# Routing of a mixture of experts: router products on tiles as they arrive, first gather ahead of the branch, a weight ring of seven

## The reference

```python
def moe_swiglu(h, w_router, b_router, w_gate, w_up, w_down):
    logits = (h @ w_router).astype(F32) + b_router.astype(F32)
    top_logits, top_idx = lax.top_k(logits, TOP_K)          # TOP_K = 2
    top_w = jax.nn.softmax(top_logits, axis=-1)
    gates = jnp.sum(jax.nn.one_hot(top_idx, N_EXPERTS, dtype=F32) * top_w[..., None], axis=-2)
    out = jnp.zeros(h.shape, F32)
    for e in range(N_EXPERTS):                              # N_EXPERTS = 8
        y_e = swiglu(h, w_gate[e], w_up[e], w_down[e]).astype(F32)   # 1024 -> 3584 -> 1024
        out = out + gates[..., e:e + 1] * y_e
    return out.astype(h.dtype)
```

## Time and profile before

| | |
|---|---|
| time, median of 3 runs | 2658.06 us (2654.54 to 2659.94) |
| profiled execution, own time | 2662.36 us |
| its span, first to last instruction | 2660.5 us |
| TensorE busy | 2539.8 us, 95% |
| VectorE, ScalarE, GpSimd busy | 72%, 55%, 7% |
| granted TensorE clock, mean over the span | 0.972 |
| memory traffic | 567.60 MB, mean 213 GB/s |

### The profile page before, as it was taken

How to read it: one execution, slowest core, us unless ns; L and a number is a source line. 1 busy time by engine, 2 the same in 40 slices (tenths; PEclk the granted TensorE clock), 3 DMA queues, 4 the chain that set the end, 5 groups by cost and what they waited for, 6 DMA issues and landing times.

```text
span 2660.5 us, 39011 instructions
## 1 busy us (share of the span) xinstructions
PE 2539.8 (95%) x15929; PEld 2257.1 (85%) x15929; DVE 1921.7 (72%) x2436; ACT 1473.6 (55%) x1801; POOL 183.8 (7%) x201
## 2 busy tenths in 40 slices
PE   7998989999989899999999999999899999898998
PEld 6766989999879788888888888888798899887998
DVE  7885366544666588989898988988775775576773
ACT  2222355434465277777777777777635564435653
POOL 0000012212010100000000000000000121100120
PEclk9988999999999999999999999999999999999999
DMA  7221044554424299999999999999762455251551
GB/s 224 85 95 48 1 153 136 190 177 158 143 66 157 67 341 381 349 351 363 367 368 333 372 361 364 350 376 360 266 199 75 143 181 184 84 186 64 187 180 46
DMA packets 339048, 567.60 MB, mean 213 GB/s; under 512 B 17576, under 2 KB 184724, under 8 KB 338740
## 3 DMA queue, kind: packets, MB, share of 16 engines
q1 hardware_dynamic: 325942, 556.29, 59.7%
q10 hardware_dynamic: 12926, 8.77, 1.2%
HBM read 563.97 MB, written 2.24 MB: 213 GB/s over the span
## 4 chain that ended last, share of the span: by engine, by line
PE 86%; DVE 7%; ACT 4%; issue 2%; ACTq 0%; DMA 0%; POOL 0%; DVEq 0%; POOLq 0%
PE bank L206 23%; PE bank L208 22%; PE bank L207 22%; PE bank L2060 3%; DVE chunks_lo L326 2%; ACT chunks_hi L318 2%; PE bank L3217 1%; PE bank L1748 1%; PE bank L1731 1%; PE bank L645 1%; PE bank L2606 1%; PE bank L2593 1%; PE bank L2607 1%; PE bank L2112 1%; PE bank L2052 1%
## 5 line engine op out<-in xcount | busy, mean ns | idle before, releaser
L3345 DVE TENSOR_TENSOR weight_lo<-ring,weight_hi 128x2048 fp32r<-128x2048 f32 x336 | 766.8, 2290 | 112.1 <-ACT weight_hi L3280 110.2
L3280 ACT ACTIVATE weight_hi<-ring 128x2048 fp32r<-128x2048 f32 x336 | 643.5, 1918 | 208.1 <-PE bank L208 204.2
L326 DVE TENSOR_TENSOR chunks_lo<-ring,chunks_hi 128x2048 fp32r<-128x2048 f32 x175 | 403.2, 2304 | 300.6 <-ACT chunks_hi L318 300.4
L206 PE MATMUL bank<-x_parts,chunks_hi 128*128 128x256 f32 x1568 | 454.8, 290 | 21.9 <-DVE x_parts L409 13.7
L318 ACT ACTIVATE chunks_hi<-ring 128x2048 fp32r<-128x2048 f32 x175 | 333.8, 1908 | 229.9 <-PE bank L208 225.4
L207 PE MATMUL bank<-x_parts,chunks_hi 128*128 128x256 f32 x1568 | 447.6, 285 | 0.0
L208 PE MATMUL bank<-x_parts,chunks_lo 128*128 128x256 f32 x1568 | 447.3, 285 | 0.0
L206 PE MATMUL bank<-weight_hi,xg_parts 128*128 128x512 f32 x896 | 353.2, 394 | 1.0 <-DVE xg_parts L3351 1.0
L208 PE MATMUL bank<-weight_hi,xg_parts 128*128 128x512 f32 x896 | 349.3, 390 | 0.0
L207 PE MATMUL bank<-weight_lo,xg_parts 128*128 128x512 f32 x896 | 349.0, 390 | 0.0
L206 PEld LDWEIGHTS bank<-x_parts,chunks_hi 128*128 128x128 f32 x1568 | 304.3, 194 | 27.1 <-issue 17.1
(11 more groups left out here) (525 smaller groups left out, 4633.8 us busy)
## 6 DMA issues: line engine op xcount, KB each, us to landing
ring<-in_moe_w_gate SPq DMA_DIRECT2D x112, 1024.0 KB, 6.8
ring<-in_moe_w_up SPq DMA_DIRECT2D x112, 1024.0 KB, 6.8
ring<-in_moe_w_down SPq DMA_DIRECT2D x112, 1024.0 KB, 6.9
ring<-in_w_up SPq DMA_DIRECT2D x44, 1024.0 KB, 5.1
ring<-in_w_in SPq DMA_DIRECT2D x24, 1024.0 KB, 5.5
ring<-in_w_down SPq DMA_DIRECT2D x22, 1024.0 KB, 4.9
ring<-in_xa_w_kv SPq DMA_DIRECT2D x16, 1024.0 KB, 5.7
ring<-in_da_w_qkv SPq DMA_DIRECT2D x12, 1024.0 KB, 5.2
```

What stands on the lines that cost most here:

```text
L206: pe.matmul(dst, l[0], r[0], start=first, stop=False, skip_group_check=True)
L326: dve.tensor_tensor(self.lo[:, n % SPLITS], ring[:, c.slot], self.hi[:, n % SPLITS].bitcast(F32), ALU.subtract).then_inc(self.rest.sem, se ...
L3280: act.activation(weight_hi[:, slot(m, odd + next_)], ring[:, m % RING], ACT.Copy)\
L3345: dve.tensor_tensor(weight_lo[:, at_], ring[:, m % RING], weight_hi[:, at_].bitcast(F32), ALU.subtract)\
```

## The change

- The router products take each scaled tile as it is ready and stand ahead of the transposes; the row sums follow them. The scaling itself moves from VectorE to ScalarE, ahead of its square (`carry_hi`).
- The four tables are loaded by ScalarE's queue after its first square of the output product.
- `end_phase()` between the routing and the experts goes. VectorE's subtraction for `xt_lo` moves behind the slots and the crowd flag. TensorE gathers the first pair, upper parts, shares, lower parts, before it loads the flag and branches; ScalarE splits two chunks and copies the gathered tokens before it does; each waits for a semaphore `crowd_known` first.
- In every pair the share products stand behind the upper gather instead of ahead of it, with one more count.
- `RING` is 7 and `SCRATCH` 2048 columns shorter. The experts use six slots (`ROUND`); the seventh holds the lower parts of the gathered tokens. GpSimd's memsets of spare columns go.

```diff
-RING = 6
+RING = 7
-        SCRATCH = 35648
+        SCRATCH = 33600
...
         def carry_hi(act, n, gain, plain):
-            if not plain:
-                act.activation(x_parts[:, 0, n], h[:, n], ACT.Copy, scale=gain(n)).then_inc(x_hi.sem, x_hi.tick())
+            act.activation(x_plain[:, n] if plain else x_parts[:, 0, n], h[:, n], ACT.Copy, scale=gain(n))\
+               .then_inc(x_hi.sem, x_hi.tick())
...
                     carry_square(act, n)
+                    if n == 0 and early is not None:
+                        early(act)
...
             def _(pe):
-                pe.wait_ge(*ready(DT - 1))
+                pe.wait_ge(consts_in.sem, consts_in.total)
+                pe.matmul(bank[6][:, 0:E], ones[0:1, :], row_b[0:1, :], start=True, stop=True)
+                for k in range(DT):
+                    pe.wait_ge(x_hi.sem, arrived + k + 1)
+                    for t in range(TT):
+                        mm = pe.matmul(bank[4 + t][:, 0:E], x[:, k, t * P:(t + 1) * P], wr[:, k], start=k == 0,
+                                       stop=k == DT - 1)
+                mm.then_inc(routed.sem, routed.tick())
+                sum_x(pe, full=False, rows=True)
                 for n in range(4):
                     t, half = divmod(n, 2)
                     for m in range(4):
                         mm = pe.transpose(bank[n][:, m * P:(m + 1) * P], x[:, 4 * half + m, t * P:(t + 1) * P], ident[:])
                     mm.then_inc(turned.sem, turned.tick())
-                pe.wait_ge(consts_in.sem, consts_in.total)
-                pe.matmul(bank[6][:, 0:E], ones[0:1, :], row_b[0:1, :], start=True, stop=True)
-                for t in range(TT):
-                    for k in range(DT):
-                        mm = pe.matmul(bank[4 + t][:, 0:E], x[:, k, t * P:(t + 1) * P], wr[:, k], start=k == 0,
-                                       stop=k == DT - 1)
-                    mm.then_inc(routed.sem, routed.tick())
-                sum_x(pe, full=False, rows=True)
                 pe.wait_ge(chosen.sem, chosen.at(1))
-                pe.wait_ge(rested.sem, rested.at(4))
...
-            end_phase()
...
-            xg_parts = take_parts("xg_parts", 2, DT, T)
+            ROUND = RING - 1
+            xg_parts = [take_parts("xg_hi", DT, T),
+                        nc.alloc_sbuf_tensor_at("xg_lo", [P, DT, T], F32R, offset=ring_at + 4 * ROUND * CHUNK)]
...
             @block.tensor
             def _(pe):
+                pair_wait(pe, one_hot, 0, 1)
+                gather(pe, 0, FIRST_HI)
+                pair_wait(pe, fetched, 0, 1)
+                shares(pe, FIRST_HI[0])
+                pe.wait_ge(rested.sem, rested.at(4))
+                gather(pe, 1, FREE)
+                pe.wait_ge(crowd_known.sem, crowd_known.at(1))
                 many = crowded(pe)
...
             @block.scalar
             def _(act):
+                act.wait_ge(turned.sem, turned.at(4))
+                for m in range(2):
+                    upper(act, 0, m, 0)
+                tokens_in(act, 0, range(4), FIRST_HI, FIRST_HI[0])
+                act.wait_ge(crowd_known.sem, crowd_known.at(1))
                 many = crowded(act)
...
             @block.vector
             def _(dve):
+                dve.wait_ge(counted.sem, counted.at(3))
+                make_slots(dve, 0)
+                ordered(dve, dve_own, dve.tensor_reduce(crowd[:, 1:2], count, AX_X, ALU.max))
+                dve.tensor_copy(crowd[:, 0:1].bitcast(mybir.dt.int32), crowd[:, 1:2]).then_inc(crowd_known.sem, crowd_known.tick())
+                for n in range(4):
+                    t, half = divmod(n, 2)
+                    c_ = slice(half * 512, (half + 1) * 512)
+                    dve.wait_ge(copied.sem, copied.at(n + 1))
+                    dve.tensor_tensor(xt_parts[1][:, t, c_], bank[n][:, :], xt_parts[0][:, t, c_].bitcast(F32), ALU.subtract)\
+                       .then_inc(rested.sem, rested.tick())
+                dve.wait_ge(crowd_known.sem, crowd_known.at(1))
                 many = crowded(dve)
```

More of the change, by code:

```diff
@@ L402, in carry_lo @@
         def carry_lo(dve, n, gain, plain):
[L404 to L407, removed]
+            if not plain:
                 dve.wait_ge(x_hi.sem, x_hi.at(n + 1))
@@ L2853, in moe @@
             eq, one, two, two_l = (take(TT, E) for _ in range(4))
-            pick_, gates_, place_ = take(TT, E + 1), take(TT, E + 1), take(TT, E + 1)
-            pick, gates, place = (v_[:, :, 0:E] for v_ in (pick_, gates_, place_))
-            scaled_gates = take(TT, E + 1)
+            pick, gates, place, scaled_gates = (take(TT, E) for _ in range(4))
             choice, share = take(TT, 2, 2), take(2, 2)
@@ L2906, in _ @@
             def _(act):
-                act.wait_ge(consts_in.sem, consts_in.total)
+                root_x(act, full=False, rows=True)
                 for n in range(4):
@@ L2932, in _ @@
                 dve.tensor_scalar(minus[:], ident[:], -1.0, None, ALU.mult)
[L2933 to L2939, removed]
+                dve.wait_ge(routed.sem, routed.at(1))
                 o(dve.tensor_copy(row_l, bank[6][:, 0:E]))
@@ L3013, in moe @@
             UP = 4 * NB
-            assert NC % RING == 0
-            per_slot = NC // RING
-            views = [ring[:, m % RING, :].rearrange("p (a b) -> p a b", a=4 if m < UP else 2) for m in range(NC)]
+            assert NC % ROUND == 0
+            per_slot = NC // ROUND
+            views = [ring[:, m % ROUND, :].rearrange("p (a b) -> p a b", a=4 if m < UP else 2) for m in range(NC)]
             one_hot, weights_hi, weights_lo, y_left, y_rest = (
@@ L3186, in gather, with shares, tokens_in, upper @@
                     mm.then_inc(gathered.sem, 1)
-            FREE, FIRST_LO = (0, 1, 2, 3), (4, 5, 6, 0)
+            def shares(pe, b):
+                for q in range(2):
+                    for t in range(TT):
+                        mm = pe.matmul(bank[b][:, 2 * q:2 * q + 2], to_slot[:, t, q * P:(q + 1) * P].bitcast(F32),
+                                       choice[:, t, q], start=t == 0, stop=t == TT - 1)
+                mm.then_inc(gathered.sem, 1)
+            FREE, FIRST_HI = (0, 1, 2, 3), (4, 5, 6, 7)
+            def tokens_in(act, pair, bs, banks, share_bank):
+                for b in bs:
+                    pair_wait(act, gathered, pair, b + 1)
+                    act.activation(xg_parts[0][:, 2 * b:2 * b + 2], bank[banks[b]][:, :].rearrange("p (a b) -> p a b", a=2),
+                                   ACT.Copy).then_inc(fetched.sem, 1)
+                if 3 in bs:
+                    pair_wait(act, gathered, pair, 5)
+                    act.activation(share, bank[share_bank][:, 0:4].rearrange("p (a b) -> p a b", a=2), ACT.Copy)\
+                       .then_inc(fetched.sem, 1)
+            def upper(act, e, m, odd, next_=0):
+                chunk_in(act, e, m, next_)
+                act.activation(weight_hi[:, slot(m, odd + next_)], ring[:, m % ROUND], ACT.Copy).then_inc(weights_hi.sem, 1)
             def to_tokens(pe, b, dst):
@@ L3232, in body @@
                                     k = 4 * half + kk
-                                    mm = three(pe, bank[(2 * b + which) % 4][:, :], [xg_parts[:, c_, k, odd * P:(odd + 1) * P] for c_ in range(2)],
+                                    mm = three(pe, bank[(2 * b + which) % 4][:, :], [x_[:, k, odd * P:(odd + 1) * P] for x_ in xg_parts],
                                                [v_[:, kk] for v_ in w], k == 0, k == DT - 1)
@@ L3406, in _ @@
                 with pe.Else():
+                    pair_wait(pe, fetched, 0, 5)
                     with pe.Fori(0, E) as e:
```

114 lines of the change are left out of this document (43 added, 71 removed).

## The result

| | before | after |
|---|---|---|
| median | 2656.72 us (2654.54 to 2664.49, 11 runs) | 2666.22 us (2657.82 to 2675.99, 11 runs) |
| profiled execution, own time | 2662.36 us | 2672.72 us |
| its span | 2660.5 us | 2670.9 us |
| clock, mean over the span | 0.972 | 0.973 |

The ratio is 1.0031 [1.0018, 1.0044]: the change made the kernel slower by 0.31%, where 2652.6 us and a gain were forecast. I cut each at three records: the start of its last output product, the start of its first expert product, and the start of its last expert product.

A forecast was written before the change was run, and what follows sets the result against it. TensorE was taken to pace the experts, with a hole of 27.5 us before them to shorten. Gain 5.7 less 0.2 for the clock gave 5.5 us, so 2652.6 us on the median's scale; range 2649.5 to 2657.0.

The forecast's parts named there:

- the seventh holds the lower tokens at another address: zero, with a rival below: Experts: keeping the lower gathered tokens in the ring's seventh slot was to cost zero.
- The slower rival: Experts: 896 stationary loads of lower tokens beside transfer writes each show 12 ns, costing 10.8 us; 2663.4 us; chance 0.05.
- The experts' start carries through one for one: Experts: TensorE paces them, so an earlier first expert product shortens the whole equally; experts' length unchanged at 976 us.
- Router products as tiles arrive: Before the routing arithmetic: bias, router products and sums fill TensorE's idle 2.01 us and pass the transposes; gain 4.00 us.
- Transposes behind, fence and branch moved: Routing: 1.97 us of transposes hidden behind VectorE's arithmetic; slots made at once, without fence and branch, gain 1.6 us.
- First gather ahead of the branch: Between slots and first expert product: gathers precede the branch, VectorE's line binds; start taken as 932.3, gain 5.7 us.
- my upper case: First gathers at half clock throughout: they end at 932.1, last copy 932.8, TensorE's own load and branch 933.1.
- The branch costs TensorE more: Before the first expert product: TensorE's bare load and branch takes 3.7 us; 2654.5, or 2657.0 us at half clock; chance 0.08.
- Clock late at both ends: Low clock from before the router products' end into the first expert products; gain 3.4 us, 2654.7 us; chance 0.21.
- Transfers take over: Experts' end hangs on the first waiting weight load, only 1.6 us earlier; gain 1.6, 2656.4 us; chance 0.06.
- The ring of seven: Weight ring outside the experts: no engine waits for a ring transfer, so a seventh slot gives zero, bound +1.0 us.
- The likeliest case's own range: Whole kernel, if the forecast of 2652.6 us (chance 0.55) holds: 2651.5 to 2653.8 us.

The follow-up runs named there:

- e3: Changed kernel with a ring of six and the lower tokens beside the upper ones, still shifted by 32 bytes: median 2651.07 us, ratio 0.997, experts 974.25 us.
- e1: Changed kernel with the dropped 32 bytes given back, lower tokens still in the seventh slot: median 2657.77 us, ratio 1.000, experts 984.00 us.
- e8: Changed kernel loading only an eighth of each expert chunk: 2674.6 us in one execution, experts 989.65 us.
- e4: Changed kernel with ring of six, tokens together and the 32 bytes restored (routing part alone): median 2648.31 us, ratio 0.9965, experts 974.31 us.
- e7: Changed kernel with ring of six, 128-byte starts, lower tokens behind the split weights: 2658.31 us in one execution, experts 974.34 us.
- e9: e4 with the lower tokens 28 KB below their place, rests still equal: 2656.55 us in one execution, experts 974.31 us.
- e2: Kernel before with 8 more unused columns (32 bytes) moving the expert tiles: median 2656.44 us, ratio 0.9996, experts 974.15 us.
- f5: Same kernel as e4, timed longer: median 2656.73 us, ratio to the kernel before 0.9978, experts 974.31 us.
- f6: Changed kernel, ring of seven, with 40 unused columns instead of 8, so all expert tiles have rest 128: median 2646.71 us, ratio to the kernel before 0.9947.
- e5: e4 with the lower tokens moved to the front of the scratch space (rest 192, others 0): 2664.0 us in one execution, experts 983.87 us.
- f4: e4 with 64 unused bytes behind the gathered tokens, shifting the weights: 2665.32 us in one execution, experts 979.61 us.
- e6: e1 with lower gathered tokens outside the ring and the not yet gathered lower parts in the seventh slot: median 2665.12 us, ratio 1.0014, experts 983.96 us.

## Why the prediction was wrong

**The step that failed** is "the seventh holds the lower tokens at another address: zero, with a rival below". It cost 15.3 us. I looked at who waits for that buffer, and nobody does. Its address as such has a price, through the rest it leaves beside the other operands'. The rests moved twice at once: the lower tokens went to 128, and the dropped spare columns took everything else to 224. The spare columns alone cost nothing (e3), the seventh slot alone 9.7 us (e1), both together 15.3.

**The slower rival** had the right place and about the right size (gate and up products, 10.8 us, 2663.4 against 2666.22), and I gave it 0.05. Its cause was wrong in two ways. The transfers have no part in it (e8). And it charged only the 896 loads of the lower tokens with 12 ns; in the kernel after all 2688 products pay, 4.6 to 7.3 by group. "Only an address changes", which I wrote against it, was the very thing.

**The experts' start carries through one for one**: right. In e4, e7 and e9 the experts have 974.3 us however early they start.

**Router products as tiles arrive.** The gain of 4.00 came to 2.1: from the last addition's start to the root 6.36 us (906.94 to 913.30), 4.4 forecast, 8.4 before. The hole and the transposes went as worked out; the clock fell at some 909.1, among the router products, which gave 1.54 back there and 0.4 at the sums. My value for this was 0.2 and my bound 1.6; the 1.9 lie beyond both. What I had not seen is that the fall's place is no property of the kernel before either: its profile had it behind the router products, but in e2, with the same routing, it lies ahead of them, among the transposes (clock 0.65 over these, 0.50 from the bias to the sums):

```profile
902.22 2.90 PE bank L2886 x16
905.13 0.52 PE bank L2889 x2
905.65 6.92 PE bank L2892 x32
912.57 0.86 PE bank L419 x4
```

There the old routing's router products take 6.92 us, and its hole 32.61 where the first profile had 27.80. The new routing's hole lies between 21.25 and 23.93 in all its profiles. I took one draw of the clock for the base.

**Transposes behind, fence and branch moved.** From the root to the slots 5.97 us were needed (913.30 to 919.27), 6.6 forecast; slots 12.3 us after the last addition, 11 forecast, 16.65 before. These steps held, and the late router products explain the rest.

**First gather ahead of the branch.** The forecast was that VectorE's line would bind, with 1.17 us of load and branch on it. In VectorE's timeline (start, duration, what) the weight rest starts before the last subtraction has ended:

```profile
921.05 2.47 DVE L3420 TENSOR_TENSOR xt_lo<-bank,xt_hi 128x512 fp32r<-128x512 f32 x4
923.44 2.28 DVE L3323 TENSOR_TENSOR weight_lo<-ring,weight_hi 128x2048 fp32r<-128x2048 f32 x1
927.31 0.69 DVE L3329 CAST xg_lo<-bank 128x512 fp32r<-128x512 f32 x1 [1.59 <-PE bank L3160]
```

Load and branch lay beside the subtractions (their records start at 921.17 and 922.08), and VectorE then waited 1.59 us for the gather. TensorE at the low clock was the line that bound, my upper case: 11.3 us from the slots to the first expert product, where that case had 11.6 and the forecast 10.8. From the last addition it is 23.6 us, 21.8 forecast. **The branch costs TensorE more**: no. Its record there took 95 ns, beside running products, and the first expert product started 0.05 us after the last copy (930.49 to 930.54).

**Clock late at both ends** (0.21) happened in front and in the gathers, but not into the experts. **Transfers take over**: no, as the waits show. **The ring of seven** gave nothing that the profiles can tell (f5 against f6: 0.4 us in the span).

So the sum for the hole, 5.5 us, was of the right size, with some luck: 3.9 between the two profiles at hand, and over all profiles the old hole has 27.8 or 32.6 us and the new one 21.3 to 23.9, depending on the clock's falls, which the sum did not see coming. The forecast fell because a term that I set to zero was nearly three times the whole sum. The range's upper end, 2657.0, stood on the rivals of the hole alone. The likeliest case's own range, up to 2653.8, was also narrower than its terms: a gain of 1.8 at worst gives 2656.3.

**What stays open.** Why a difference of rests costs TensorE time, up to 7.3 ns a product, and why a shift of the weights by 64 bytes costs little more than a third of one by 32 or 128, is not shown: the traces have no record of the reads themselves. It is also open which of the three products pays in which case. With only the lower tokens at another rest, the product of the two upper parts kept its distance at a difference of 128 bytes (e1: 227.2 ns, the other two 232.3 and 234.1), and paid like the others at 192 bytes (e5: 231.9, 231.0, 230.7) and at 96 (the kernel after). Neither the rests of a product's own two operands nor those of the next load against the running product sort these cases. Equal rests were without a price in every run; the size of the price at unequal ones is a table, not yet a rule.

## What to carry to other kernels

Where TensorE is the bound and such products (fp32r, 512 columns; nothing else was tried) stream back to back, keep the start addresses of all stationary and moving tiles equal modulo 256 bytes, and fix them explicitly: a tile moved for capacity, or a spare column dropped, can cost more than the edit brings. When a changed kernel's long stage grows with no new wait, compare the distance from start to start of its products before looking for a story about queues or transfers. And treat the clock's falls in one profile as one draw: compare kernels on executions whose stretch ahead of the edit has the same length.

## What the runs showed of the hardware

- Products of 512 columns in fp32r with a 128 by 128 stationary operand stand 227 to 228 ns apart where all tiles have equal rests modulo 256 bytes (rests 0, 32, 128 and 224 tried), and in most cases 230 to 235 where they have not (differences of 32, 64, 96, 128 and 192 bytes tried; the exceptions are two groups at 228.2 and 229.7 with 64 bytes, in f4, and one at 227.2 with 128, in e1 and e6). Their weight loads show 188 ns either way.
- The wider spacing, 233 ns in the kernel after, is there beside an idle ScalarE and beside an idle VectorE alike.
- Taking the transfers from 353 to 51 GB/s changed the experts by 0.06 us of 989.6.
- The granted clock fell behind the 8-column router products in the profile of the kernel before, some 2 us into them in the kernel after, and ahead of them in e2, whose program differs from the kernel before by 32 spare bytes. The fronts of the profiles form two groups, 898.3 to 900.2 us with 48 to 55 us at the lower level, and 906.6 to 910.2 us with 72 to 79.
